# A hybrid recurrent decoder trunk: each dense slice as five products instead of six, with the prompt's 512 columns in one

## The reference, cut to what matters

```
u = xn @ w['ab_w_in'][j]                                            # layer 0: 2048 -> 7200
y = jnp.concatenate([o_dn, o_gla], axis=-1) @ w['ab_w_out'][j]      # 2048 -> 2048
gate = jax.nn.sigmoid(_rmsnorm(h, w['ple_norm'][li]) @ w['ple_w_gate'][li])
h = h + gate * (p[li] @ w['ple_w_proj'][li])
...
u = xn @ w['cd_w_in'][j]                                            # layer 1
y = jnp.concatenate([y_ssd, y_lru], axis=-1) @ w['cd_w_out'][j]
```

## Time and profile before

| | |
|---|---|
| median of 3 runs | 2507.78 us (2507.23 to 2509.1) |
| span of the profiled execution | 2502.7 us |
| TensorE busy with products | 2426.0 us, 97% |
| TensorE busy with weight loads | 2298.4 us, 92% |
| VectorE, ScalarE, GpSimd busy | 50%, 38%, 15% |
| mean granted TensorE clock | 0.991 |

### The profile page before, as it was taken

One profiled execution on the slowest core, in us unless ns is written; L12 is line 12 of the kernel. 1 busy time (PEld: TensorE's weight loads), 2 busy tenths in 40 slices (PEclk: granted clock), 3 DMA queues, 4 the chain that ended last, 5 costly groups with the idle time before them and its releaser, 6 DMA issues.

```text
span 2502.7 us, 52615 instructions
## 1 busy us (share of the span) xinstructions
PE 2426.0 (97%) x22783; PEld 2298.4 (92%) x22783; DVE 1254.3 (50%) x2301; ACT 951.4 (38%) x1531; POOL 367.3 (15%) x558
## 2 busy tenths in 40 slices
PE   7999999999999999999999999999999999999996
PEld 7998889888889999989999999988899999999996
DVE  6644655545544554732253456466656562243332
ACT  5423444234433343432252243244445552243222
POOL 3101101110100010111111111122212121111111
PEclk9999999999999999999999999999999999999998
DMA  9333333333343543653233333233323354323232
GB/s 244 98 103 98 110 96 107 88 96 97 114 118 96 157 142 94 202 172 89 85 99 99 109 99 100 73 91 87 84 80 107 90 162 148 87 83 94 77 87 74
DMA packets 375543, 271.30 MB, mean 108 GB/s; under 512 B 24419, under 2 KB 346733, under 8 KB 374800
## 3 DMA queue, kind: packets, MB, share of 16 engines
q1 hardware_dynamic: 341424, 172.53, 25.5%
q0 software_dynamic: 22080, 72.77, 9.0%
q10 hardware_dynamic: 11808, 22.63, 2.6%
HBM read 220.24 MB, written 48.37 MB: 107 GB/s over the span
## 4 chain that ended last, share of the span: by engine, by line
PE 88%; DVE 4%; ACT 4%; DMA 2%; issue 2%; SPq 0%; ACTq 0%; POOL 0%; DVEq 0%; POOLq 0%
PE psd L570 71%; PE psw L593 2%; PE psw L592 2%; PE psw L620 1%; PE psw L670 1%; PE psw L648 1%; DVE arena L1965 1%; DMA w_raw<-in_ab_w_in_dram 1%; PE psw L656 1%; PE psw L642 1%; DMA mix<-in_x_prompt_dram 1%; ACT w_hi L1137 1%; PE psw L662 0%; PE psw L634 0%; PE psw L970 0%
## 5 line engine op out<-in xcount | busy, mean ns | idle before, releaser
L570 PE MATMUL psd<-xh,w_hi 128*128 128x272 f32 x5056 | 1107.0, 300 | 15.7 <-DVE xl L1741 6.5
L570 PE MATMUL psd<-xh,w_lo 128*128 128x272 f32 x5056 | 1048.5, 289 | 0.4 <-issue 0.4
L570 PE MATMUL psd<-xl,w_hi 128*128 128x272 f32 x5056 | 1046.2, 288 | 0.0
L570 PEld LDWEIGHTS psd<-xh,w_hi 128*128 128x128 f32 x5056 | 797.4, 189 | 71.0 <-issue 37.9
L570 PEld LDWEIGHTS psd<-xl,w_hi 128*128 128x128 f32 x5056 | 797.2, 189 | 0.0
L570 PEld LDWEIGHTS psd<-xh,w_lo 128*128 128x128 f32 x5056 | 793.2, 189 | 0.0
L1681 DVE TENSOR_TENSOR w_lo<-w_raw,w_hi 128x512 fp32r<-128x512 f32 x632 | 434.5, 705 | 403.4 <-ACT w_hi L1137 402.0
L1137 ACT CAST w_hi<-w_raw 128x512 fp32r<-128x512 f32 x632 | 377.2, 615 | 576.6 <-PE psd L570 513.6
L2560 POOL TENSOR_TENSOR states<-states,extra 128x544 f32<-128x544 f32 x59 | 80.0, 1355 | 524.6 <-ACT extra L1192 524.6
L2366 DVE TENSOR_TENSOR extra<-psd,rstd 128x544 f32<-128x544 f32 x32 | 23.2, 724 | 156.3 <-PE psd L570 139.2
L2345 DVE TENSOR_TENSOR arena<-arena,psd 128x544 f32<-128x544 f32 x32 | 23.0, 720 | 133.5 <-PE psd L570 127.1
(11 more groups left out here) (513 smaller groups left out, 2377.9 us busy)
## 6 DMA issues: line engine op xcount, KB each, us to landing
w_raw<-in_ab_w_in_dram SPq DMA_DIRECT2D x224, 256.0 KB, 3.0
w_raw<-in_cd_w_in_dram SPq DMA_DIRECT2D x148, 256.0 KB, 3.0
w_raw<-in_ple_w_gate_dram SPq DMA_DIRECT2D x128, 256.0 KB, 3.1
w_raw<-in_ab_w_out_dram SPq DMA_DIRECT2D x64, 256.0 KB, 2.9
w_raw<-in_cd_w_out_dram SPq DMA_DIRECT2D x64, 256.0 KB, 3.0
uT_scratch<-mix ACTq DMA_DIRECT2D x53, 272.0 KB, 2.4
hT_scratch<-arena POOLq DMA_DIRECT2D x8, 1088.0 KB, 5.6
arena<-hT_scratch POOLq DMA_DIRECT2D x8, 1088.0 KB, 9.3
```

The costliest lines, as they stand in the source:

```text
L570: mm = pe.matmul(out[:, D0 + HALF * half:D0 + HALF * (half + 1)], w[:, r, k % QH, :], x[:, k, HALF * half:HALF * (half + 1)], start=(k == ...
```

## The change

The columns of a slice are cut in another way. Activations move to one tensor `xhl[P, KT, 2, T]` that holds the high and low part of a slice side by side, so that one access can take the 32 sample columns of both. A slice is then

1. `w_hi` times the 512 prompt columns of `xh`,
2. `w_hi` times 64 columns: the 32 sample columns of `xh` and those of `xl`, into two places of PSUM (512 to 543 and 544 to 575),
3. `w_hi` times the 512 prompt columns of `xl`,
4. `w_lo` times the 32 sample columns of `xh`, added to the first of the two places,
5. `w_lo` times the 512 prompt columns of `xh`.

The columns streamed are 512+64+512+32+512 = 1632 as before (6 x 272). The samples' sum now lies in two places, so VectorE has to add them when it takes the tile out: four instructions in place of one for 126 tiles, three in place of one for the 32 tiles of the output projections.

```diff
-HALF = T // 2
-D0 = SEQ - HALF
+XS = SEQ + NS
...
-        xh, xl = sb("xh", [P, KT, T], F32R), sb("xl", [P, KT, T], F32R)
+        xhl = sb("xhl", [P, KT, 2, T], F32R)
+        xh, xl = xhl[:, :, 0, :], xhl[:, :, 1, :]
...
-                for i, (w, x) in enumerate(((w_hi, xh), (w_hi, xl), (w_lo, xh))):
-                    for half in range(2):
-                        mm = pe.matmul(out[:, D0 + HALF * half:D0 + HALF * (half + 1)], w[:, r, k % QH, :],
-                                       x[:, k, HALF * half:HALF * (half + 1)],
-                                       start=(k == 0 and i == 0), stop=(k == KT - 1 and i == 2))
+                hi, lo = w_hi[:, r, k % QH, :], w_lo[:, r, k % QH, :]
+                begin, end = k == 0, k == KT - 1
+                pe.matmul(out[:, 0:SEQ], hi, xh[:, k, 0:SEQ], start=begin, stop=False)
+                pe.matmul(out[:, SEQ:XS + NS], hi, xhl[:, k, :, SEQ:T], start=begin, stop=end)
+                pe.matmul(out[:, 0:SEQ], hi, xl[:, k, 0:SEQ], start=False, stop=False)
+                pe.matmul(out[:, SEQ:XS], lo, xh[:, k, SEQ:T], start=False, stop=end, skip_group_check=True)
+                mm = pe.matmul(out[:, 0:SEQ], lo, xh[:, k, 0:SEQ], start=False, stop=end)
                 mm.then_inc(S["slice_done"], 1)
...
+            def scaled_tile(dst, d):
+
+                W, more = psd[d % 2], smp_lo[:, NS * (d % 2):NS * (d % 2) + NS]
+                go(dve.tensor_tensor(more, W[:, XS:XS + NS], rstd[:, SEQ:T], ALU.mult))
+                go(dve.tensor_tensor(dst[:, SEQ:T], W[:, SEQ:XS], rstd[:, SEQ:T], ALU.mult))
+                dve.tensor_tensor(dst[:, 0:SEQ], W[:, 0:SEQ], rstd[:, 0:SEQ], ALU.mult)
+                wait_chain()
+                dve.tensor_tensor(dst[:, SEQ:T], dst[:, SEQ:T], more, ALU.add).then_inc(S[f"dense_read{d % 2}"], 1)
+
...
-                dve.tensor_tensor(dst, psd[d % 2][:, D0:D0 + T], rstd[:, :], ALU.mult)\
-                   .then_inc(S[f"dense_read{d % 2}"], 1)
+                scaled_tile(dst, d)
...
-                    dve.tensor_tensor(hT(c), hT(c), psd[d % 2][:, D0:D0 + T], ALU.add)\
-                       .then_inc(S[f"dense_read{d % 2}"], 1)
+                    W, h, more = psd[d % 2], hT(c), smp_lo[:, NS * (d % 2):NS * (d % 2) + NS]
+                    go(dve.tensor_tensor(more, h[:, SEQ:T], W[:, XS:XS + NS], ALU.add))
+                    dve.tensor_tensor(h[:, 0:SEQ], h[:, 0:SEQ], W[:, 0:SEQ], ALU.add)
+                    wait_chain()
+                    dve.tensor_tensor(h[:, SEQ:T], more, W[:, SEQ:XS], ALU.add).then_inc(S[f"dense_read{d % 2}"], 1)
...
-                    dve.tensor_tensor(e, psd[d % 2][:, D0:D0 + T], rstd[:, :], ALU.mult)\
-                       .then_inc(S[f"dense_read{d % 2}"], 1)
+                    scaled_tile(e, d)
```

More of the change, by code:

```diff
@@ L254, in trunk @@
         wa2 = sb("wa2", [P, GLA_KW])
+        smp_lo = sb("smp_lo", [P, 2 * NS])
         C32 = c32[:, 0:6 * 32].rearrange("p (l j) -> p l j", l=6)
```

## The result

The changed kernel takes 2899.43 us (median of 4 runs, 2896.93 to 2901.15) against 2507.62 us (2507.23 to 2509.1). The ratio is 1.156, with a 95% interval of 1.155 to 1.158. The span of the profiled execution went from 2502.7 to 2894.8 us, +392.1.

What follows compares the result with a forecast made beforehand. TensorE was taken as the bound, at 88% of the chain. Span 2502.7 + 410 (slices) + 3 (VectorE) - 15 (waits) = 2901 us; with 5.1 us from span to median, 2906 us, range 2790 to 3010.

Steps and rivals of the forecast that it cites:

- The narrow products: Products 2 and 4 of a slice: each lasts as long as the next weight load, 112 ns, 224 for both.
- one ahead, not two: On TensorE, a weight load begins when the product before its own begins, never earlier; a 128x128 load takes about 111 ns.
- The wide products: Products 1, 3 and 5 of a slice, 512 columns each: 230 ns each, 690 ns for three.
- a fixed and a proportional reading: For 512 columns: 225 ns if the extra 12 ns is fixed per product, 235 if it goes with the columns.
- The upper end of 242: Highest price of a 512-column product in ns, from a line through 118 and 133 ns; gives +501 us.
- The waits given back: TensorE's waits at slices and three group lines, together 35 us, get more cover from longer slices: 15 us back.
- VectorE: Added instructions when tiles are taken out: 75 us more work, +3 us of time at the last tiles of phases.
- The clock: TensorE's granted clock was expected to stay full; a fall to 1.2 GHz for long stretches was given 2%.
- The rival: TensorE's clock falls to 1.2 GHz for long stretches, streaming doubles: about 880 us more, 3800 us; chance 2%.
- The page of the Trainium skill: Load and product pairs on TensorE at 131 and 81 ns: 555 ns a slice, a time near 2010 us.
- the rival with deeper loads: On TensorE, loads run two ahead and hide under wide products: 730 ns a slice, about 2450 us; chance 6%.

Runs made afterwards that it cites:

- `mixed_loads`: Kernel before plus test products behind its last one, wide products given fewer weight columns: wide-narrow pairs took 0.34, 0.29 and 0.26 us with 128, 64 and 32.
- `curve`: Kernel before plus blocks of test products of many widths and types behind its last one: F32R took 204 ns at 448 columns, 111 at 128.
- `joint288`: Changed kernel with the column cut at 288 instead of 512, still five products a slice: 2522.95 us, 1.006 of the kernel before.
- alternating pairs: Test products behind the last one of the kernel before, F32R of 512 columns in turn with 32: 0.34 us a pair.

## Why the prediction was right

Forecast 2906 us, measured 2899; the range was 2790 to 3010. The mechanism, narrow products that last as long as the next load, is what the runs show. That the number is only 7 us off is in part luck, as the terms below say.

- **The narrow products** were put at 112 ns each from rows 4 and rows 6. They cost 108, and `mixed_loads` shows that it is the load for the product behind. The step that carried the forecast, "one ahead, not two", holds: with deeper loads the load of line 575 would have begun soon after 1500.23, when the unit was free, and not at 1500.36.
- **The wide products** were put at 230 ns, between a fixed and a proportional reading. The proportional one (235) was nearly right: about 234 in the changed kernel (919 less 2 x 108, by three), 233 without narrow products. The wide products came out 4 ns dearer, three times in a slice, the narrow ones 4 ns cheaper, twice: 914 was forecast, 919 measured, +422 us instead of +410. The upper end of 242 does not follow from its rows: a line through 118 ns at 256 and 133 at 288 columns gives 238 at 512. The range's upper bound was that much too high, which changes nothing here.
- **The waits given back** were put at 15 us and came to some 30, with what VectorE adds set off against them. The two errors, +12 and -18, happen to cancel for the most part.
- **VectorE** was put at +3 us; alone it costs about 5. Its busy time rose by 44 us, not 75, since its short instructions overlap.
- **The clock** stayed at 2.4 GHz as much as before, with 24 us at 1.2 in either kernel before the last 30. The rival was not empty: in `curve` the clock fell in a run of narrow products alone. Why it did not fall in the changed kernel, no run here shows.
- **The page of the Trainium skill** (TensorE: Matmul & The Clock Gate, Back-to-back issue gap) with 131 ns for 512 columns and 81 for 128 would have given 555 ns a slice. No run here shows these distances: F32R gave 234 and 111, and bf16 already 164 at 384 columns, while at 128 columns a bf16 product took (2.0 - 0.219) / 31 = 57 ns, less than the page says. The 81 ns alone would not have carried the rival with deeper loads, which needs under 62 ns for both narrow products: with wide products at 230 ns the slice would be 690 + 2 x 81 = 852 ns.

## What to carry to other kernels

Count a product on TensorE as the larger of its own streaming and the load of the *next* weights; a narrow product between wide ones pays the next load in full, however much time the wide ones had to spare. In `joint288` one product fewer gained nothing, since all of them already streamed longer than a load; so cut columns so that none streams for less than that, rather than to the full width. And check what each type costs: in this kernel a small term in bf16 is cheaper to stream and to load than in F32R.

## What was not expected of the hardware

- F32R does not stream at one column a cycle of 2.4 GHz: 204 ns at 448 columns, 176 at 384, against 187 and 160. bf16 does (164 at 384). Why is open. The load beside it does not explain it, and other engines neither: in the alternating pairs, with no other engine at work, 512 columns take 234 ns against 213.
- A 128x128 load takes 108 to 112 ns in F32R and at most 29 ns in bf16. At a granted clock of 1.2 GHz the F32R load takes 214.
- Every second bf16 element, read in place from F32R values, costs a slice only 8 ns more (737 against 729) than packed copies: 3 for the weights, 5 for the activations.
